# Expert weights in six transfers of 2 MB instead of twelve of 1 MB, with the rows of each dealt to the partitions to suit

## The reference, cut to what matters

```python
logits = xt @ w_router + b_router                 # xt: 256 x 1024, 32 experts
top_val, top_idx = lax.top_k(logits, 4)
gates = jax.nn.softmax(top_val, axis=-1)
# for each expert e and the tokens that chose it:
gu = xb @ w_gate_up[e] + b_gate_up[e]             # 1024 -> 2048
x_glu = jnp.minimum(gu[:, :1024], 7.0)
x_lin = jnp.clip(gu[:, 1024:], -7.0, 7.0)
act = (x_lin + 1) * (x_glu * jax.nn.sigmoid(1.702 * x_glu))
y = act @ w_down[e] + b_down[e]                   # 1024 -> 1024
acc = acc.at[tok].add(y * g[:, None])
```

## Time and profile before

| | |
|---|---|
| time, median of 3 runs | 1198.87 us (1197.37 to 1198.95) |
| span of the profiled execution | 1195.7 us (no separate total is listed for it) |
| PE busy | 1136.8 us, 95% |
| PEld busy | 501.2 us, 42% |
| DVE busy | 319.0 us, 27% |
| ACT busy | 192.5 us, 16% |
| POOL busy | 139.6 us, 12% |
| moved by DMA | 436.96 MB, mean 365 GB/s |

### The profile page before, as it was taken

The page is one execution under the profiler, slowest core; times in us unless marked ns, Lnnn a source line. Parts: engine busy times, 40 slices in busy tenths (PEclk is TensorE's granted clock), DMA queues, the critical chain, the costliest instruction groups (busy, mean ns, idle before and its releaser), DMA issues.

```text
span 1195.7 us, 14434 instructions
## 1 busy us (share of the span) xinstructions
PE 1136.8 (95%) x5601; PEld 501.2 (42%) x5602; DVE 319.0 (27%) x539; ACT 192.5 (16%) x318; POOL 139.6 (12%) x76
## 2 busy tenths in 40 slices
PE   8988899999999999999999999999999999999996
PEld 7987898633333333333333333333333333333332
DVE  4664422322222222222222222222222222222223
ACT  6522444200000000000000000000000000000002
POOL 6756765100000000000000000000000000000000
PEclk9989999999999999999999999999999999999998
DMA  9943645699999999999999999999999999999980
GB/s 328 354 142 119 232 147 210 238 416 355 417 416 419 417 418 417 417 417 418 418 417 418 418 418 417 418 418 417 418 418 418 417 418 417 418 417 418 417 347 36
DMA packets 93263, 436.96 MB, mean 365 GB/s; under 512 B 6865, under 2 KB 23313, under 8 KB 60433
## 3 DMA queue, kind: packets, MB, share of 16 engines
q1 hardware_dynamic: 93072, 436.13, 90.8%
q0 software_dynamic: 160, 0.41, 0.1%
HBM read 435.46 MB, written 1.05 MB: 365 GB/s over the span
## 4 chain that ended last, share of the span: by engine, by line
PE 90%; DVE 5%; ACT 4%; issue 1%; DMA 1%; SPq 0%; DVEq 0%; ACTq 0%
PE ps L676 37%; PE ps L708 19%; PE ps L496 6%; PE ps L719 5%; PE ps L469 5%; PE ps L667 5%; PE ps L652 5%; PE ps L697 3%; ACT y_sb L770 2%; ACT actT L770 2%; PE ps L692 2%; DVE win L1032 1%; PE ps L684 1%; DMA ring<-in_w_v 1%; PE ps L598 1%
## 5 line engine op out<-in xcount | busy, mean ns | idle before, releaser
L676 PE MATMUL ps<-ring,xT 128*64 128x512 f32 x2032 | 443.3, 594 | 0.0
L676 PEld LDWEIGHTS ps<-ring,xT 128*64 128x64 f32 x2032 | 143.1, 137 | 297.8 <-issue 297.8
L708 PE MATMUL ps<-ring,actT 128*64 128x512 f32 x1024 | 226.8, 595 | 8.0 <-ACT actT L770 8.0
L1226 DVE TENSOR_TENSOR h_rows<-ps,h_rows 128x1024 f32<-128x1024 f32 x64 | 75.4, 1219 | 271.4 <-PE ps L719 271.4
L421 POOL TENSOR_TENSOR w_lo<-ring,w_hi 128x1024 fp32r<-128x1024 f32 x56 | 135.6, 2422 | 73.2 <-PE ps L469 37.0
L1213 DVE TENSOR_SCALAR glu<-ps 128x512 f32<-128x512 f32 x32 | 22.1, 692 | 421.2 <-PE ps L676 421.2
L708 PEld LDWEIGHTS ps<-ring,actT 128*64 128x64 f32 x1024 | 70.7, 137 | 143.5 <-issue 127.9
L915 ACT ACTIVATE sig<-glu 128x512 f32<-128x512 f32 x32 | 20.2, 630 | 593.0 <-DVE glu L1213 593.0
L719 PE MATMUL ps<-y_sb,g_sb 64*128 64x512 f32 x256 | 63.6, 615 | 22.3 <-ACT y_sb L770 22.3
L770 ACT ACTIVATE w_hi<-ring 128x1024 fp32r<-128x1024 f32 x56 | 59.1, 1058 | 84.6 <-PE ps L469 47.8
L652 PE MATMUL ps<-n_rows,sel 128*64 128x512 f32 x264 | 62.3, 592 | 0.0
(11 more groups left out here) (174 smaller groups left out, 746.7 us busy)
## 6 DMA issues: line engine op xcount, KB each, us to landing
ring<-in_w_gate_up SPq DMA_DIRECT2D x254, 1024.0 KB, 11.3
ring<-in_w_down SPq DMA_DIRECT2D x128, 1024.0 KB, 13.7
ring<-in_w_in SPq DMA_DIRECT2D x8, 1024.0 KB, 12.1
ring<-in_w_v SPq DMA_DIRECT2D x4, 1024.0 KB, 12.9
ring<-in_w_k SPq DMA_DIRECT2D x4, 1024.0 KB, 5.0
ring<-in_w_out SPq DMA_DIRECT2D x4, 1024.0 KB, 10.4
ring<-in_w_q SPq DMA_DIRECT2D x4, 1024.0 KB, 4.9
ring<-in_w_o SPq DMA_DIRECT2D x4, 1024.0 KB, 4.9
```

The source lines that it names most:

```text
L676: mm = pe.matmul(ps[CAP * half:CAP * (half + 1), bank, :], lhsT, w[:, bank * D + half * HALF:bank * D + (half + 1) * HALF], start=False, s ...
L708: mm = pe.matmul(ps[CAP * half:CAP * (half + 1), bank_y, :], lhsT, w[:, a * D + half * HALF:a * D + (half + 1) * HALF], start=False, stop= ...
L1226: dve.tensor_tensor(h_rows[:, t, :].rearrange("p (a n) -> p a n", a=2), ps[:, b:b + 2, :], h_rows[:, t, :].rearrange("p (a n) -> p a n", a ...
```

## The change

One expert's weights now come in six transfers of 2 MB: four of gate and up, two of down. Every transfer brings each partition one unbroken run of 16 KB. For gate and up, partition p gets rows 8p to 8p+7 of the matrix over the four transfers, two rows in each; a run begins 64 KB after that of the partition before. For down, each transfer takes one half of 512 rows, and partition p gets its rows 4p to 4p+3; the transfer is one solid stretch of 2 MB.

A product adds up over partitions, so the other operand has to follow. ScalarE writes `n_rows` with element 8p+k of a token at place 128k+p, so that the gathered and turned tokens have it at partition p; the gain is loaded once more in that order (`gain_moe`, a transfer of its own with the semaphore `gain_in`). The transposes of `act` take every fourth column as weights in place of 128 adjacent ones, so that actT has element 4p+r of a half at partition p.

The ring has 8 units of 2 MB and one spare, the same 18 MB together. Some tiles move (`hn_hi`, `gT` and `gfin` to unit 22, `w_hi` and the activation tiles to unit 18) so that the spare's two units adjoin. TensorE waits and signals six times for each expert instead of twelve; a unit of 2 MB is given back once both its halves are used. The diff, cut to its core:

```diff
-RING = 16
 FRONT_RING = 10
 CHUNK = 2048
+BIG = 2 * CHUNK
+RING = 8
 UNROLL = 4
-PER_EXPERT = 12
+GATE_UP, DOWN = 4, 2
+PER_EXPERT = GATE_UP + DOWN
-SLOT_ORDER = (10, 8, 9, 13, 0, 1, 2, 3, 14, 15, 4, 5, 12, 6, 7, 11)
-EXTRA = 2
+SLOT_ORDER = (4, 0, 1, 7, 2, 6, 3, 5)
+EXTRA = 1
...
-            if c < 8:
-                return w_gate_up[0, bass.ds(e, 1), P * c:P * (c + 1), :].rearrange("o p n -> p (o n)")
-            return w_down[0, bass.ds(e, 1), 256 * (c - 8):256 * (c - 7), :].rearrange("o (a p) n -> p (o a) n", p=P)
+            if c < GATE_UP:
+                return w_gate_up[0, bass.ds(e, 1), :, :].rearrange("o (p k) n -> p (o k n)", k=KC)[:, BIG * c:BIG * (c + 1)]
+            half = w_down[0, bass.ds(e, 1), HALF * (c - GATE_UP):HALF * (c - GATE_UP + 1), :]
+            return half.rearrange("o (p r) n -> p (o r n)", r=4)
...
+            sp.dma_start(gain_moe[:], g_moe[0].rearrange("(p k) -> p k", k=KC)).then_inc(gain_in, 16)
             for n, slot in enumerate(SLOT_ORDER):
-                if slot == 10:
+                if slot == 5:
                     sp.wait_ge(mixed, 8)
-                elif slot == 13:
-                    a_complete(sp, "k3")
-                elif slot == 14:
+                    sp.wait_ge(halves_used, 2 * FRONT)
+                elif slot == 6:
+                    a_complete(sp, "o3")
+                elif slot == 7:
                     a_complete(sp, "s3")
+                    b, uses = t_use("P3")
+                    sp.wait_ge(t_full[b], uses)
                     sp.dma_start(bgu_sb[:], b_gate_up[0]).then_inc(bgu_in, 16)
                     sp.dma_start(bdn_sb[:], b_down[0]).then_inc(bdn_in, 16)
...
                 else:
-                    last = max(q for q in range(FRONT) if q % FRONT_RING == slot)
+                    last = max(q for q in range(FRONT) if q % FRONT_RING == 2 * slot + 1)
                     sp.wait_ge(w_lo_ok, 2 * (last + 1))
...
+            a_complete(sp, "logits")
+            sp.dma_start(extra[:], expert_source(RING // PER_EXPERT, RING % PER_EXPERT)).then_inc(extra_full, 16)
...
-                for k in range(KC):
-                    w = wait_chunk(k)
-                    lhsT = xT[par][:, (k % 4) * P + CAP * (k // 4):(k % 4) * P + CAP * (k // 4 + 1)]
...
+                for c in range(GATE_UP):
+                    w = wait_chunk(c)
+                    for a in range(2):
+                        k = 2 * c + a
+                        lhsT = xT[par][:, (k % 4) * P + CAP * (k // 4):(k % 4) * P + CAP * (k // 4 + 1)]
...
                     mm.then_inc(chunks_used, 1)
...
-                    mm = pe.transpose(ps[:, bank_t[1], j * P:(j + 1) * P], act[:, j * P:(j + 1) * P], ident[:])
+                    mm = pe.transpose(ps[:, bank_t[1], j * P:(j + 1) * P], act[:].rearrange("s (p r) -> s r p", r=4)[:, j, :], ident[:])
...
-                for c in range(8, PER_EXPERT):
-                    w = wait_chunk(c)
+                for h in range(DOWN):
+                    w = wait_chunk(GATE_UP + h)
+                    for r in range(4):
+                        lhsT = actT[:, r * P + CAP * h:r * P + CAP * (h + 1)]
...
-                act_e.activation(n_rows[:, c, :], h_rows[:, c, :], ACT.Copy, scale=stat[:, 3, 2, c:c + 1]).then_inc(scaled, 1)
+                act_e.activation(n_rows[:, c, :].rearrange("t (k p) -> t k p", p=P),
+                                 h_rows[:, c, :].rearrange("t (p k) -> t k p", p=P), ACT.Copy,
+                                 scale=stat[:, 3, 2, c:c + 1]).then_inc(scaled, 1)
...
-                gain = vec[:, ROW_MOE:ROW_MOE + KC].rearrange("p (h j) -> p j h", h=2).unsqueeze(3).broadcast_to([P, 4, 2, CAP])
+                gain = gain_moe[:].rearrange("p (h j) -> p j h", h=2).unsqueeze(3).broadcast_to([P, 4, 2, CAP])
...
+            dve.wait_ge(gain_in, 16)
             tokens_out(0, 0)
```

More of the change, by code:

```diff
@@ L119, in program @@
         v_rows = at("v_rows", 21, [P, TC, D])
-        w_hi = [at(f"w_hi{i}", unit, [P, CHUNK // 2], F32R) for i, unit in enumerate((22, 22.5, 11, 11.5))]
+        w_hi = [at(f"w_hi{i}", unit, [P, CHUNK // 2], F32R) for i, unit in enumerate((18, 18.5, 11, 11.5))]
         w_lo = [at(f"w_lo{i}", 23 + 0.5 * i, [P, CHUNK // 2], F32R) for i in range(LO_BUFS)]
@@ L130, in program @@
         g_sb = at("g_sb", 19, [P, SEQ], skip=3 * HALF)
-        glu, lin, sig, act = (at(n, 22, [P, HALF], skip=HALF * i) for i, n in enumerate(("glu", "lin", "sig", "act")))
-        h_squares = at("h_squares", 22, [P, TC, D])
+        glu, lin, sig, act = (at(n, 18, [P, HALF], skip=HALF * i) for i, n in enumerate(("glu", "lin", "sig", "act")))
+        h_squares = at("h_squares", 18, [P, TC, D])
         bgu_sb = at("bgu_sb", 20, [E, 2 * D])
         actT, y_sb = at("actT", 21, [P, HALF]), at("y_sb", 21, [P, HALF], skip=HALF)
-        extra = [at("extra0", 23, [P, CHUNK]), at("extra1", 18, [P, CHUNK])]
-        gfin = at("gfin", 18, [P, D])
+        extra = at("extra", 22, [P, BIG])
+        gfin = at("gfin", 22, [P, D])
         bdn_sb = at("bdn_sb", 24, [E, D])
@@ L148, in program @@
         vec = sb("vec", [P, N_ROWS])
+        gain_moe = sb("gain_moe", [P, KC])
         wp_sb = sb("wp_sb", [P, GROUPS, P])
@@ L172, in program @@
         bank_xg, bank_y = 2, 3
-        slot_full = [sem(f"slot_full{i}") for i in range(RING)]
-        extra_full = [sem(f"extra_full{i}") for i in range(EXTRA)]
+        slot_full = [sem(f"slot_full{i}") for i in range(FRONT_RING)]
+        big_full = [sem(f"big_full{i}") for i in range(RING)]
+        extra_full = sem("extra_full")
+        gain_in = sem("gain_in")
         x_in = [sem("x_in0"), sem("x_in1")]
@@ L246, in expert_chunk @@
         def expert_chunk(eng, n, turn=None):
-            if turn is None and RING <= n < RING + EXTRA:
-                eng.wait_ge(extra_full[n - RING], 16)
-                return extra[n - RING][:]
+            if turn is None and n == RING:
+                eng.wait_ge(extra_full, 16)
+                return extra[:]
             m = ring_place(n) if turn is None else n - EXTRA
             slot = SLOT_ORDER[m % RING]
-            have = 16 * (front_uses[slot] + m // RING + 1)
-            eng.wait_ge(slot_full[slot], have if turn is None else turn * (16 * BODY // RING) + have)
-            return ring[:, slot, :]
+            have = 16 * (m // RING + 1)
+            eng.wait_ge(big_full[slot], have if turn is None else turn * (16 * BODY // RING) + have)
+            return big[:, slot, :]
         others = [n for n in A_USES if n[0] not in "uCvBkq"]
@@ L362, in stream @@
                 sp.wait_ge(chunks_used, turn * BODY + (before + 1))
[L363 to L364 removed]
+                sp.dma_start(big[:, slot, :], expert_source(turn * UNROLL + n // PER_EXPERT, n % PER_EXPERT)) \
+                    .then_inc(big_full[slot], 16)
             most = load_most(sp)
@@ L380, in load_again @@
                     slot = SLOT_ORDER[c]
-                    sp.dma_start(as_target(ring[:, slot, :], c), expert_source(e, c)).then_inc(slot_full[slot], 16)
+                    sp.dma_start(big[:, slot, :], expert_source(e, c)).then_inc(big_full[slot], 16)
             more_rounds(sp, most, load_again)
@@ L670, in gate_up @@
                 pe.wait_ge(xT_ok, s + ahead)
-                for k in range(KC):
-                    w = wait_chunk(k)
-                    lhsT = xT[par][:, (k % 4) * P + CAP * (k // 4):(k % 4) * P + CAP * (k // 4 + 1)]
[L674 to L678, removed]
+                for c in range(GATE_UP):
[3 more added lines that the diff above has]
+                        lhsT = xT[par][:, (k % 4) * P + CAP * (k // 4):(k % 4) * P + CAP * (k // 4 + 1)]
+                        for bank in range(2):
+                            for half in range(2):
+                                mm = pe.matmul(ps[CAP * half:CAP * (half + 1), bank, :], lhsT,
+                                               w[:, a * CHUNK + bank * D + half * HALF:a * CHUNK + bank * D + (half + 1) * HALF],
+                                               start=False, stop=(k == KC - 1), skip_group_check=True)
                     mm.then_inc(chunks_used, 1)
@@ L701, in down @@
                 pe.wait_ge(aT_ok, s + 1)
-                for c in range(8, PER_EXPERT):
-                    w = wait_chunk(c)
-                    for a in range(2):
-                        k = 2 * (c - 8) + a
-                        lhsT = actT[:, (k % 4) * P + CAP * (k // 4):(k % 4) * P + CAP * (k // 4 + 1)]
+                for h in range(DOWN):
+                    w = wait_chunk(GATE_UP + h)
+                    for r in range(4):
+                        lhsT = actT[:, r * P + CAP * h:r * P + CAP * (h + 1)]
                         for half in range(2):
                             mm = pe.matmul(ps[CAP * half:CAP * (half + 1), bank_y, :], lhsT,
-                                           w[:, a * D + half * HALF:a * D + (half + 1) * HALF], start=False,
```

(7 more changed lines are left out.)

32 lines of the change are left out of this document (7 added, 25 removed).

## The result

The changed kernel takes 1200.62 us (median of 12 runs, 1199.92 to 1201.64) against 1198.22 us for the kernel before (median of 12 runs, 1197.04 to 1198.95). The ratio is 1.0022 with a 95% interval of 1.0013 to 1.0030: slower by 2.4 us, little but clear of no change, as the interval lies above 1.

What follows compares the result with a forecast made beforehand. The prediction took TensorE with two ScalarE copies as the bound, at 29.88 us per expert, not DMA. Its terms, 0 + 0 + 0, left the span at 1195.7 us and the time at 1198.9, range 1195 to 1213.

Steps and rivals of the forecast that it cites:

- What bounds it: Expert stage: TensorE and two ScalarE copies set 29.88 us per expert; transfers wait for TensorE, not the other way round.
- Removed waits: Matmuls of an expert: six of twelve TensorE waits removed, taken as 0 gain, 4 us at most; faster rival's chance 0.06.
- The turned activation: Four transposes loading act at a step of four floats: taken as 0, range end 14.1 us, 42 us at four times.
- The sign that I gave for slow loads: Trace of act's four loads: 0.6 to 0.85 us instead of 0.42, with 30.1 or 30.3 us between expert biases.
- The argument for 0: Turned activation: the router's products suggest loads need only about 1.2 floats per ns, leaving some room, so cost 0.
- Gather and n_rows: ScalarE's permuted n_rows copies before the gather, 2.6 us of cover: 0 up to double time; late-start rival +4 us, chance 0.02.
- Gain, first loads, ring: Extra 4 KB gain transfer, first expert's weight loads and steady-state buffer reuse: all early enough, cost 0.
- The lead: Ring in steady state: 22 us or more of slack, so any mean DMA rate above 411 GB/s costs nothing.
- DMA's speed: Expert weight transfers: longer pieces should not be worse than 417 to 418 GB/s; even 3% more buys nothing.
- the 64 KB pitch: Rival on gate-up transfers, 16 KB from every 64 KB slowing DMA: +47 us at 380 GB/s, +102 at 352; chance 0.07.
- What lies around the span: Outside the profiled span: 3.2 us between span 1195.7 and median time 1198.87, carried over unchanged.
- The strided load: Rival at turn_act: strided weight loads of act slow the kernel by 7.0 to 14.1 us, 1206 to 1213; chance 0.17.

Runs made afterwards that it cites:

- the early-bias kernel: The kernel before with the next expert's gate-up biases issued ahead of scatter: 1180.40 us, ratio 0.9841.
- the two kernels with halves: The kernel before and the changed kernel, each with gate-up and down products on 256 of each 512 columns: 1173.29 us and 1151.46 us.

## Why the prediction was right or wrong

*What bounds it.* Right. The distance between experts is set by TensorE and its two ScalarE copies in both kernels, and by no transfer; a DMA faster by 2.5% bought nothing until TensorE's work was cut.

*Removed waits, taken at 0 with 4 us at most.* Right: with the step taken out, the changed kernel stands at 0.9998 and 0.9997, intervals that hold 1. Gate-up is 13.88 us as before with half the waits.

*The turned activation, taken at 0.* This is the step that failed. It costs 0.090 us per expert, 2.9 us in all, and is the whole difference. My bounds held it, but their working was off: I had the case "half as long again" at 7.0 us, and the load did become 1.5 times as long (140 to 212 ns). I had let the pace of the transposes grow as the load does, four times 0.055 us. Measured, the first of each four grew by 54 ns and the others by 12 each: three of the four loads are mostly hidden beside a transpose. The sign that I gave for slow loads, four of them in 0.6 to 0.85 us, was too high for the same reason; they stand at 0.56. The argument for 0, that 1.2 floats per ns leaves room, was drawn from adjacent reads and says nothing of stepped ones; its figure was off as well, for the router's rows give 128/0.115 = 1.1, and the load itself takes 140 ns, 0.9. That the sum came within 2 us of the measured time owes something to luck: nothing in that argument kept the load's price as small as it is. Of the Trainium skill's note (SBUF — State Buffer, "Door 1: The DMA port swizzle") neither half agrees with these runs: a stride of four fp32 is not free (212 ns against 140), and two hits in a line don't restore full rate (210).

*Gather and n_rows.* Right as to cost, by its own margin: I gave it 0 up to double and 4 us from four times on; the two copies took 4.21 for 2.19 us, 1.9 times, and were covered.

*Gain, first loads, ring.* Right: no wait of TensorE for a landing in the expert stage. One reading was off without harm: I had the loading of expert weights begin near 133.6 us, and it begins at 144.9 (timeline of SP's queue), 85 us before the first is wanted:

```profile
144.91 33.01 SPq L346 DMA_DIRECT2D big<-in_w_gate_up  x3
```

The lead, which I put at 22 us or more for the 2 MB units, is some 27 for the ring of 1 MB units, by the early-bias kernel; for the 2 MB units, DMA at 422 GB/s (29.8 us per expert) against 29.12 falls behind by 31 x 0.7 = 21 us, which used it up to a first wait of 0.6 us at the last expert, so that 22 was about right there.

*DMA's speed.* Right in sign: the 64 KB pitch does no harm (428 GB/s). The Trainium skill's row on pitches (DMA: Bandwidth & Descriptors, "Latency and other measured facts"), where 512 KB still ran 207 of 214 GB/s, gives nothing for 64 KB; that a smaller pitch is harmless, as the prediction took from it, fits these runs.

*What lies around the span.* The 3.2 us were the median of three runs less the span of one of them. A run's time is 1.7 to 1.9 us above its own span in every run of the two kernels whose span is on record. The forecast of no change doesn't rest on it, since it stands on both sides.

*The rivals.* The strided load came true at less than half of its lower price. As to the sign I gave no change 0.66 and slower 0.26; the time lies inside my band for no change (1196.5 to 1201.3), but the ratio of 1.0022 is just past the 0.2% that I set, and its interval is above 1: the rival that I gave 0.17 is what happened, at a smaller size.

## What to carry to other kernels

Before making transfers faster, read who waits for them: DMA busy over 90% in nearly every slice can still be the one that waits, and then transfers 2.5% faster are worth nothing, while each nanosecond added to the chain of the engine that sets the pace is paid once per expert, 32 times. Of a longer weight load only what runs beside nothing is paid in full: 54 ns of the first here, 12 of each that follows. A layout that suits the transfers moves a permutation somewhere; price it on the engine that ends up doing it, and look for a split (here gate-up in long runs, down as it was) in which none is needed. Once TensorE was relieved of 0.77 us per expert, the faster transfers did become worth some 5 us: such a change is tried again after the bound has moved.

## What the runs showed of the hardware

- A weight load of 128 float columns takes 140 ns adjacent, 210 at a step of two floats, 212 at four, 192 at eight (another tile). In a group of four transposes the step of four adds 54 ns with the first and 12 with each of the others.
- ScalarE's copy of 128x1024 floats takes 1.14 us adjacent and 2.15 reading at a step of eight; VectorE's product of 128x512 takes 0.69 adjacent and 1.05 with both inputs at a step of four and the output scattered.
- DMA moves 418 GB/s in runs of 8 KB (gate-up) and 4 KB (down), 422 in runs of 16 and 4 KB, and 428 to 429 in runs of 16 KB, each with its line full.
- With DMA setting the pace, one issue of a 1 MB transfer held SP for 1.0 us (gate-up, median) and 4.1 us (down) and up to 7.0, while one of 2 MB in runs of 16 KB took 0.33 us every time, though the median from issue to landing was 23 us in the first case and 36 in the second (from 700 to 1000 us of the two kernels with halves).
- The early bias gained 0.77 us per expert, more than the 0.70 of idle time that it fills: scatter then follows other products without a stop and takes 1.92 instead of 1.99 us.
